# Boundaries of a two-layer decoder trunk: squares summed on the tensor engine, earlier token sums, residual tiles finished one by one, and the upper part of x led into the products

## The reference

```
def rmsnorm(x, g):
    y = xf * lax.rsqrt(jnp.mean(xf * xf, axis=-1, keepdims=True) + RMS_EPS)
    return (y * g.astype(jnp.float32)).astype(x.dtype)

for layer in range(2):
    h = rmsnorm(x, g[0]);  m = mixer(h)
    x = x + rmsnorm(m, g[1])
    h = rmsnorm(x, g[2])
    x = x + rmsnorm(cross_attn(h, mem, xa_wq, xa_wkv, xa_wo), g[3])
    h = rmsnorm(x, g[4])
    x = x + rmsnorm(sq_relu_mlp(h, mlp_w1, mlp_w2), g[5])
```

## Time and profile before

| | us |
|---|---|
| Median of 3 runs | 994.5 |
| Lowest and highest | 993.26, 994.54 |
| Profiled execution, its own time | 995.42 |
| Its span | 993.5 |
| PE busy in it | 926.3 (93%) |
| DVE busy | 668.4 (67%) |
| ACT busy | 472.1 (48%) |
| POOL busy | 315.3 (32%) |
| From issue to landing of a 512 KB unit, median | 3.7 to 3.9 |

### The profile page before, as it was taken

The page is one execution under the profiler, slowest core; times in us unless marked ns, Lnnn a source line. Parts: engine busy times, 40 slices in busy tenths (PEclk is TensorE's granted clock), DMA queues, the critical chain, the costliest instruction groups (busy, mean ns, idle before and its releaser), DMA issues.

```text
span 993.5 us, 17155 instructions
## 1 busy us (share of the span) xinstructions
PE 926.3 (93%) x7268; PEld 899.3 (91%) x7268; DVE 668.4 (67%) x1013; ACT 472.1 (48%) x660; POOL 315.3 (32%) x213
## 2 busy tenths in 40 slices
PE   5978988989999999999989998999998889999997
PEld 5878987879898999999989998889998789999996
DVE  6796497686648655455588999986586385544553
ACT  4443444454546444444454433636465364444443
POOL 3242482542324100000158877536441330000000
PEclk8998999999999999999999999999999989999999
DMA  8443532455354555665555555335542435565551
GB/s 269 136 128 99 177 107 65 148 161 159 106 170 148 190 172 174 202 186 184 188 148 170 182 180 157 100 107 169 170 149 75 138 122 175 173 198 188 186 190 44
DMA packets 81031, 153.74 MB, mean 155 GB/s; under 512 B 6251, under 2 KB 7227, under 8 KB 80955
## 3 DMA queue, kind: packets, MB, share of 16 engines
q1 hardware_dynamic: 80843, 152.60, 48.7%
q10 hardware_dynamic: 112, 0.05, 0.0%
HBM read 151.58 MB, written 1.05 MB: 154 GB/s over the span
## 4 chain that ended last, share of the span: by engine, by line
PE 70%; DVE 20%; ACT 3%; issue 3%; POOL 2%; DMA 1%; DVEq 0%; POOLq 0%; ACTq 0%
PE ps L496 21%; PE ps L498 21%; PE ps L497 21%; DVE ps L1618 5%; DVE w_lo L1263 3%; DVE xc L1332 2%; POOL w_lo L1891 1%; PE ps L735 1%; PE ps L737 1%; PE ps L736 1%; ACT w_hi L919 1%; DVE xc L1329 1%; PE ps L563 1%; DVE E L1480 1%; DVE cv L1781 1%
## 5 line engine op out<-in xcount | busy, mean ns | idle before, releaser
L919 ACT ACTIVATE w_hi<-raw 128x1024 fp32r<-128x1024 f32 x284 | 296.9, 1055 | 282.4 <-DMA raw<-in_mlp_w 146.7
L496 PE MATMUL ps<-h_hi,w_hi 128*128 128x256 f32 x1280 | 370.8, 290 | 30.9 <-issue 12.9
L497 PE MATMUL ps<-h_lo,w_hi 128*128 128x256 f32 x1280 | 368.1, 288 | 0.0
L498 PE MATMUL ps<-h_hi,w_lo 128*128 128x256 f32 x1280 | 367.7, 287 | 0.0
L1263 DVE TENSOR_TENSOR w_lo<-raw,w_hi 128x1024 fp32r<-128x1024 f32 x192 | 250.5, 1324 | 136.8 <-ACT w_hi L919 136.6
L1891 POOL TENSOR_TENSOR w_lo<-raw,w_hi 128x1024 fp32r<-128x1024 f32 x92 | 229.6, 2510 | 188.4 <-ACT w_hi L919 188.4
L496 PEld LDWEIGHTS ps<-h_hi,w_hi 128*128 128x128 f32 x1280 | 251.7, 197 | 35.6 <-issue 21.5
L497 PEld LDWEIGHTS ps<-h_lo,w_hi 128*128 128x128 f32 x1280 | 251.9, 197 | 0.0
L498 PEld LDWEIGHTS ps<-h_hi,w_lo 128*128 128x128 f32 x1280 | 251.7, 197 | 0.0
L1914 POOL TENSOR_TENSOR rfac<-stat,mhalf 128x2 f32<-128x2 f32 (+1 forms) x14 | 16.5, 1181 | 428.0 <-DVE stat L1548 334.3
L498 PE MATMUL ps<-r_hi,w_lo 128*128 128x256 f32 x512 | 143.8, 281 | 0.0
(11 more groups left out here) (247 smaller groups left out, 1322.7 us busy)
## 6 DMA issues: line engine op xcount, KB each, us to landing
raw<-in_mlp_w SPq DMA_DIRECT2D x128, 512.0 KB, 3.8
raw<-in_cd_w_in SPq DMA_DIRECT2D x40, 512.0 KB, 3.7
raw<-in_xa_wkv SPq DMA_DIRECT2D x32, 512.0 KB, 3.8
raw<-in_ab_w_in SPq DMA_DIRECT2D x24, 512.0 KB, 3.8
raw<-in_xa_wq SPq DMA_DIRECT2D x16, 512.0 KB, 3.9
raw<-in_xa_wo SPq DMA_DIRECT2D x16, 512.0 KB, 3.8
raw<-in_cd_w_out SPq DMA_DIRECT2D x16, 512.0 KB, 3.9
raw<-in_ab_w_out SPq DMA_DIRECT2D x12, 512.0 KB, 3.7
```

Source lines behind the costliest of these rows:

```text
L496: nc.tensor.matmul(dst, wt[0], x[0], start=start, stop=False, skip_group_check=True)
L497: nc.tensor.matmul(dst, wt[0], x[1], start=False, stop=False, skip_group_check=True)
L498: return nc.tensor.matmul(dst, wt[1], x[0], start=False, stop=stop, skip_group_check=True)
L919: nc.scalar.activation(w_hi[:, v % SLOTS, :, :], raw[:, v % SLOTS, :, :], ACT.Copy)\
```

## The change

It touches the five boundaries and nothing else.

- **Squares.** DVE adds only the first three squares into `Ssum` (which stays two halves wide); the fourth stays in `sq`. PE takes all four half tiles of both for each of the two token groups: 8 products with a column of ones, 4 of `Ssum` and 4 of `sq`, where it had 2 of `S2`. DVE's last addition and its fold go away.
- **One filler unit sooner.** In PE's order the token sums stand behind F0 (before, behind F1), and the row of the factor behind F1 (before, behind F2).
- **ACT's order.** The third square no longer stands behind the rounding of unit F3 (of W2 and W3 in E), and with a filler `Nrow` stands behind W1 only, not behind W2. W2 and W3 are rounded between the tiles of the new x.
- **Residual tiles.** DVE makes x of tile j right behind its tmp (before, tmp ran one tile ahead), and the lower part follows one tile later. With a filler the lower part of W2, which had stood before the first tile, now stands between tiles 6 and 7.
- **hi products lead.** In W0's first tile, PE runs the 8 products that need only `h_hi` and waits for `h_lo` behind them.

```diff
...
+                        if hi_first and kt == 0:
+                            hi_first()
+                            x_hi, x_lo = src(0)
+                            for n in range(4):
+                                if n % 2 == 0:
+                                    acquire(dest[n // 2])
+                                w = unit_w(u, 0, n)
+                                dst = bank2(dest[n // 2])[:, n % 2, :]
+                                nc.tensor.matmul(dst, w[0], x_hi, start=(n % 2 == 0), stop=False, skip_group_check=True)
+                                nc.tensor.matmul(dst, w[1], x_hi, start=False, stop=False, skip_group_check=True)
+                            ready(0)
+                            for n in range(4):
+                                nc.tensor.matmul(bank2(dest[n // 2])[:, n % 2, :], unit_w(u, 0, n)[0], x_lo,
+                                                 start=False, stop=False, skip_group_check=True)
+                            continue
...
+            def h_hi_ready(tag):
+                return lambda: pe.wait_ge(act_made, after("act", "h", tag, 0))
...
             def boundary(l, n, filler):
 
 
-                filler([0, 1])
-                pe.wait_ge(dve_made, after("dve", "S2", l, n))
-                token_sums(("nstat", l, n), halves(S2))
-                filler([2])
+                filler([0])
+                nst = ("nstat", l, n)
+                acquire(nst)
+                for i, src in enumerate((Ssum, sq[:, 1, :])):
+                    if i == 0:
+                        pe.wait_ge(dve_made, after("dve", "Ssum3", l, n))
+                    else:
+                        pe.wait_ge(act_made, after("act", "nsq", l, n, 3))
+                    for c in range(2):
+                        for t in range(TT):
+                            mm = nc.tensor.matmul(bank(nst)[:, t:t + 1], src[:, c * T + t * P:c * T + (t + 1) * P],
+                                                  ones[:, 0:1], start=(i == 0 and c == 0 and t == 0),
+                                                  stop=(i == 1 and c == 1), skip_group_check=True)
+                mm.then_inc(*finish(nst))
+                filler([1])
                 pe.wait_ge(pool_made, after("pool", "nr", l, n))
                 rows(("nrow", l, n), [rfac[:, 1 + 3 * l + n, t:t + 1] for t in range(TT)])
-                filler([3])
+                filler([2, 3])
...
-                project(("q", l, 0), [("q", l, 0, 0), ("q", l, 0, 1)], h_src, ready=h_ready(f"q{l}"), tail=0)
+                project(("q", l, 0), [("q", l, 0, 0), ("q", l, 0, 1)], h_src, ready=h_ready(f"q{l}"), tail=0,
+                        hi_first=h_hi_ready(f"q{l}"))
...
                         act.wait_ge(*full(m[i]))
                         if i >= 2:
-                            act.wait_ge(dve_made, after("dve", "Ssum", l, n, 1 if i == 2 else 2))
+                            act.wait_ge(dve_made, after("dve", "Ssum", l, n))
                         nc.scalar.activation(sq[:, i % 2, :].rearrange("p (c t) -> p c t", c=2), bank2(m[i]),
                                              ACT.Square).then_inc(act_made, tick("act", "nsq", l, n, i))
-                        if i == 1:
-                            round_to(x + 3)
+                        if i == 1 and fill:
+                            round_to(x + 2)
+                    round_to(x + 3 if fill else x + 2)
                     if fill:
-                        round_to(nxt + 2)
+                        round_to(nxt + 1)
                     act.wait_ge(*full(("nrow", l, n)))
                     nc.scalar.activation(Nrow[:, :], bank(("nrow", l, n))[:, 0:T], ACT.Copy)\
                         .then_inc(act_made, tick("act", "Nrow", l, n))
                     freed("act", ("nrow", l, n))
-                    round_to(nxt + 3)
                     if tag:
                         new_h(tag, gl, gs, nxt)
...
-            def new_x(l, n, m, tag, gl, gs):
+            def new_x(l, n, m, tag, gl, gs, nxt):
 
                 dve.wait_ge(act_made, after("act", "Nrow", l, n))
-                for j in range(J + 2):
+                for j in range(J + 1):
                     if j < J:
                         if j >= 2:
                             dve.wait_ge(dve_made, after("dve", "x", tag, j - 2))
@@ -1561,24 +1592,33 @@
                                                op1=ALU.mult).then_inc(dve_made, tick("dve", "dx", l, n, j))
                         if j % 2 == 1:
                             freed("dve", m[j // 2])
-                    if 1 <= j <= J:
-                        dve.wait_ge(dve_made, after("dve", "dx", l, n, j - 1))
-                        V.tensor_tensor(xT[:, j - 1, :], xT[:, j - 1, :], tmp[:, (j - 1) % 2, :], ALU.add)\
-                            .then_inc(dve_made, tick("dve", "x", tag, j - 1))
-                    if j >= 2:
-                        low_h(tag, gl, gs, j - 2)
+                        dve.wait_ge(dve_made, after("dve", "dx", l, n, j))
+                        V.tensor_tensor(xT[:, j, :], xT[:, j, :], tmp[:, j % 2, :], ALU.add)\
+                            .then_inc(dve_made, tick("dve", "x", tag, j))
+                    if j >= 1:
+                        low_h(tag, gl, gs, j - 1)
+                    if j == 3:
+                        low_to(nxt + 1)
+                    if j == 6:
+                        low_to(nxt + 2)
 
             def boundary(l, n, m, tag, gl, gs, nxt):
 
                 fill = FILL.get((l, n))
                 x = nxt - 4 if fill else nxt
                 low_to(x + 1 if fill else x)
-                norm_sum(l, n, m)
+                dve.wait_ge(act_made, after("act", "nsq", l, n, 1))
+                V.tensor_tensor(Ssum[:, :], sq[:, 0, :], sq[:, 1, :], ALU.add)\
+                    .then_inc(dve_made, tick("dve", "Ssum", l, n))
+                dve.wait_ge(act_made, after("act", "nsq", l, n, 2))
+                own()
+                V.tensor_tensor(Ssum[:, :], Ssum[:, :], sq[:, 0, :], ALU.add)\
+                    .then_inc(dve_made, tick("dve", "Ssum3", l, n))
                 if fill:
-                    low_to(nxt - 1)
+                    low_to(nxt - 2)
                 factor(l, n)
-                low_to(nxt + 2)
-                new_x(l, n, m, tag, gl, gs)
+                low_to(nxt if fill else nxt + 2)
+                new_x(l, n, m, tag, gl, gs, nxt)
...
```

7 lines of the change are left out of this document (4 added, 3 removed).

## The result

The changed kernel takes 1004.5 us (median of 16 runs, 1000.39 to 1007.17) where the kernel before, on the same chip, took 994.5 (16 runs): the ratio is 1.0073, 95% interval 1.0047 to 1.0098, so it is slower by 0.7%, about 7 us. The two medians are 10.0 us apart, more than the ratio says: the runs of the kernel before are spread widely (990.14 to 1002.90), and the interval, 5 to 10 us, tells more than one figure. The profiled executions span 1001.4 and 993.5 us, so 7.9 more.

The account below looks back on a forecast made before the run. PE, 93% busy, was taken as the bound, so gains must come from its idle or slow time. Boundary terms -0.4 + 0.7 + 2.3 + 0.4 + 0.1 gave +3.1 us, taken as +2.5: 997.0 us, range 988 to 1004.5.

Parts of the forecast that it names:

- rival 2: In front of W2: POOL first in every meeting, 3.9 us stall, clock falls each time; +11.9 us, 1006.4; chance 15%.
- The gap goes, the wait stands in front of W2: First four boundaries: no gap in front of W0, instead PE stalls 2.4 us in front of W2.
- t: Start of DVE's tmp of tile 0 in each boundary, 5.1 us before PE reaches W0; 296.1 in the second boundary.
- `w_lo` of W2 at t + 13.2: DVE, behind tile 6: lower part of W2 ends then, while PE wants it at t + 10.8; stall 2.4 us.
- `h_lo` of tile 4 follows it directly: DVE: this goes right behind x5, ending at t + 10.0, ahead of POOL's addition.
- The clock falls in 0.6 of the cases: PE behind the stall in front of W2: 0.6 of a 1.7 us clock loss, taken as 1.0 us.
- Tile by tile is hidden: DVE's residual tiles: about 1.25 us each instead of 1.12, covered by PE's 1.4 per tile.
- C has no clock loss to win back and loses most: Third boundary: it kept 2.4 GHz before, so its next token sums come 2.3 us later.
- E gives back what it wins: Fifth boundary: 3.6 us won at W0's start are given back by the end of W3; net +0.1 us.
- Only the boundaries were added up: Total over the five boundaries: their changes sum to +3.1 us, taken as +2.5.

Follow-up runs that it names:

- w2_early: Changed kernel with both halves of W2 made ahead of tile 0 again, as before the change: 995.7 us, ratio 0.9993 to the kernel before.
- w3_early: Changed kernel with W3's upper half rounded on ACT right behind the row's copy, W2's `w_lo` staying behind tile 6: 1011.1 us, ratio 1.0140 to the kernel before.
- before_tiles: Kernel before with the tile-by-tile loop alone, W2's `w_lo` staying ahead of tile 0: 1000.4 us, ratio 1.0038.
- tiles_old: Changed kernel with the old loop, tmp one tile ahead, W2's `w_lo` still behind x of tile 6: 991.1 us, ratio 0.9952 to the kernel before.
- tiles_sums: Changed kernel with the old overlapping tile loop and the squares summed on DVE again: 990.4 us, ratio 0.9946 to the kernel before.
- w3_on_dve: Changed kernel with `w_lo` of W3 made by DVE behind tile 7 and not by POOL: 992.1 us, ratio 0.9965 to the kernel before.
- combo: Changed kernel with the old overlapping tile loop and both halves of W2 ahead of tile 0 again: 993.9 us, ratio 0.9973 to the kernel before.
- best: combo with the squares summed on DVE and, in the fifth boundary, W3 rounded before the row's copy: 988.3 us, ratio 0.9910 to the kernel before.
- tiles_sums_w3: tiles_sums with `w_lo` of W3 made by DVE behind tile 7 and not by POOL: 988.9 us, ratio 0.9938 to the kernel before.

## Why the prediction came out as it did

The direction was right, and so was the kind of mechanism: the gap in front of W0 turns into a wait for the `w_lo` of W2. The forecast itself was not: its time was 7.5 us too low (1004.5 measured, 997.0 predicted), and what happened is rival 2, to which I had given 15%. Its sign, the granted clock low behind all four stalls, stands in the rows above, and it gave +1.9, +2.5, +4.3, +2.7 and +0.5 where +1.5, +2.4, +4.4, +2.2 and +0.4 were measured, +11.9 against +10.8 together. The spans differ by less, 7.9, because of the 3.3 us that this profile wins in the layer norm, which no sum had. That 1004.5 is still inside the range, whose end is 1004.5, is luck.

- *The gap goes, the wait stands in front of W2.* Right: shown by the rows and by w2_early.
- *t.* Predicted 8.0 us behind F0 in B, measured 8.4. The 0.4 is mostly the sums on PE, 1.65 us and not 1.4: +1.0 us over four boundaries.
- *`w_lo` of W2 at t + 13.2.* The step that failed is "`h_lo` of tile 4 follows it directly". POOL's first addition started at 307.31, while the held x 5 had not ended (307.63), and went ahead of `h_lo` 4, and the second went ahead of `h_lo` 5. That is t + 14.2 and a wait of 3.1 to 3.6 us, not 2.4: +4 us. The Trainium skill, page "SBUF — State Buffer", section "Who interferes with whom", gives the shared pair to whoever issues first for the whole instruction; I weighed it and set x 7 of the earlier trace rows against it. The three held instructions of B agree with the page, and one row was too few to overrule it. The trace of the kernel before had a second case for the page in the same stretch: x 5, which started at 306.14 behind POOL's addition of 305.44, took 1.12 us and not 0.41.
- *The clock falls in 0.6 of the cases.* It fell in four of four, behind waits of 3.1 us and more: +2.8 us. That the length settles it is not shown: 2.98 us did not bring it down in B of w3_early, and in before_tiles C's gap of 2.13 did, where the 2.12 of the earlier trace rows had not. Where the wait was under 2 us or gone (tiles_old, tiles_sums, w3_on_dve, combo, w2_early) it stayed up in front of and behind W2.
- *Tile by tile is hidden.* Wrong as a cost. I priced the 0.13 us per tile and found PE's 1.4 us above it, but did not price that the order decides which DVE instructions meet POOL. Taken back it shortens A to D by 12.9 us, clock falls included (tiles_old); alone in the kernel before it costs 0.4% (before_tiles). The prediction had only its 1 us inside t + 13.2.
- *C has no clock loss to win back and loses most.* Right: the largest of the four, +4.4 where +2.3 was given.
- *E gives back what it wins.* Right: W0 comes 57.2 us behind D's token sums instead of 60.1, so 2.9 sooner (3.6 predicted), and E's own token sums come 0.4 later (0.1 predicted), where PE waits 1.43 us for POOL's fold, as the prediction had it. A second part it did not have: the granted clock is low until 5.8 us behind the start of W0 and no longer until 3.3, which is about 1.3 us.
- *Only the boundaries were added up.* The sums treat what lies between two boundaries as fixed. For the changed kernel that is so within 0.4 us, but for the layer norm; for the kernels without the long wait in front of W2 it is not, and the attention behind D takes back up to 3 us.

What stays open: whether combo or tiles_old is faster; what the earlier sums and row, the leading hi products and the rounding of W3 are worth each, since best keeps them together; whether the wait in the attention behind D goes when DVE's queue there is made shorter; what decides in a single meeting, since x 7 in the earlier trace rows did pass an addition issued 0.29 us ahead of it while `h_lo` 3 of before_tiles, 0.02 us behind one, did not; and how often the layer norm's fold is hit over many runs, for a timed run shows no rows.

## What to carry to other kernels

When a gap in front of a projection is closed, list what had been prepared inside that gap: here `w_lo` of W2 had been free work before tile 0, and behind tile 6 it became the next wait. An order of small instructions on one engine is not priced by its own sum while another engine can hold it up; count the meetings, and take the engine that starts first to win each, as it did here but for x 7 of the earlier trace rows and the start shown at the same time in tiles_old. When an engine stops waiting, look further down for who was using that wait: by the rows of the attention behind D, DVE had caught up while PE stood in front of W2. And when some of five edits are good, try them with the others taken back: the parts that gained here were hidden under those that cost more.

## What the runs showed of the hardware

- Beside POOL's `w_lo` or additions, a held DVE instruction that reads two operands from SBUF ends about 0.3 us behind POOL's end, whatever its own length: 2.67 us for a 0.42 us addition, 1.51 for a 0.47 us `h_lo`. tmp, with one operand in PSUM, was not held (two in 0.88 us beside POOL's `w_lo`). But a TENSOR_SCALAR of 128x2 that reads one operand from SBUF was: 2.35 us instead of 0.17 (w2_early).
- A start 0.01 us behind POOL's is enough to be held (x 5, 304.96 against 304.95), and one shown at the same 304.27 was not (x 5 in tiles_old). So a few hundredths decide which instruction is held: in tiles_old it was the next one, `h_lo` 4, for 2.61 us.
- Eight float32 products of a 128x128 tile with a single column of ones are 16 records and keep PE for 1.65 us, about 0.10 a record, near the 0.12 us of a 256-column product in fp32r.
- The length of a wait does not by itself say whether the clock falls: 1.95 (tiles_sums) and 1.84 (tiles_old) did not bring it down and 1.75 did (tiles_sums_w3); 2.12 did not in the earlier trace rows and 2.13 did at the same place in before_tiles; 2.98 did not in w3_early. Behind the same two waits of 1.24 to 1.25 and 0.63 us, in the attention of layer 0, it fell in five of fourteen profiles.
